# A hybrid encoder layer: the MLP's ticks taken in pairs, two strips and then four projections

## The reference, cut to what matters

```
hn = rmsnorm(x, ln1_g) * (1.0 + sc1) + sh1
z = hn @ w_in
...
o_c = stick_breaking(qc, k_all, v_all, q_pos, k_pos).reshape(b, t, GROUP_W)
...
mix = jnp.concatenate([o_a, o_b, o_c, o_d], axis=-1) @ w_out
x = x + g1 * mix
h2 = rmsnorm(x, ln2_g) * (1.0 + sc2) + sh2
x = x + g2 * (jnp.square(jax.nn.relu(h2 @ mlp_w1)) @ mlp_w2)
...
y_prompt = rmsnorm(xp, final_g)
```

## Time and profile before

| | |
|---|---|
| median of 3 runs | 3203.18 us |
| the profiled execution | 3203.64 us |
| its span, first to last instruction | 3201.8 us |
| mean granted clock of TensorE | 0.928 |
| TensorE busy | 2816.2 us (88%), 15463 matmuls |
| ScalarE, VectorE, GpSimd busy | 1556.1, 1355.5, 1718.6 us |
| last phase | from about 1100 us to the end |

### The profile page before, as it was taken

How to read it: one execution, slowest core, us unless ns; L and a number is a source line. 1 busy time by engine, 2 the same in 40 slices (tenths; PEclk the granted TensorE clock), 3 DMA queues, 4 the chain that set the end, 5 groups by cost and what they waited for, 6 DMA issues and landing times.

```text
span 3201.8 us, 41705 instructions
## 1 busy us (share of the span) xinstructions
PE 2816.2 (88%) x15463; PEld 2509.3 (78%) x15463; DVE 1355.5 (42%) x2145; ACT 1556.1 (49%) x2711; POOL 1718.6 (54%) x1063
## 2 busy tenths in 40 slices
PE   5898998998982469897899988899999989999998
PEld 1676776766461369887898988899899989999998
DVE  1262544534112426653566644566566323223222
ACT  2345454534233426653566644566567534434443
POOL 2335354443321036554665656566556666776775
PEclk8999999998975579998999999999999999999999
DMA  5236353444835234435345444545345454555542
GB/s 202 64 92 184 92 159 118 128 116 135 267 94 137 65 96 132 119 110 155 108 139 151 123 141 142 154 135 166 108 132 146 127 170 137 156 153 143 151 135 84
DMA packets 680334, 429.62 MB, mean 134 GB/s; under 512 B 38491, under 2 KB 637894, under 8 KB 680134
## 3 DMA queue, kind: packets, MB, share of 16 engines
q1 hardware_dynamic: 678054, 422.76, 45.2%
q10 hardware_dynamic: 2080, 4.19, 0.4%
HBM read 375.17 MB, written 51.59 MB: 133 GB/s over the span
## 4 chain that ended last, share of the span: by engine, by line
PE 43%; DVE 9%; ACT 5%; POOL 5%; issue 3%; DMA 2%; SPq 1%; DVEq 0%; ACTq 0%; POOLq 0%
PE t_hp L2249 7%; PE t_hp L2253 7%; PE t_hp L2250 7%; PE t_op L2280 6%; PE t_op L2282 6%; PE t_op L2281 6%; POOL t_w1l L1847 3%; DVE t_cc L2059 3%; PE t_tr L2193 1%; DVE t_lt L2058 1%; DMA t_h_lo<-o_scratch 1%; POOL t_nacc L1861 1%; DVE t_xs L2146 1%; ACT t_lt L1922 1%; DMA t_kt<-k_scratch 1%
## 5 line engine op out<-in xcount | busy, mean ns | idle before, releaser
L1847 POOL TENSOR_TENSOR t_w1l<-t_raw,t_w1h 128x1024 fp32r<-128x1024 f32 x240 | 583.6, 2432 | 644.8 <-ACT t_w1h L1942 644.5
L2249 PE MATMUL t_hp<-t_h_hi,t_w1h 128*128 128x352 f32 x1920 | 633.9, 330 | 50.4 <-DMA t_h_lo<-o_scratch 30.2
L1853 POOL TENSOR_TENSOR t_w2l<-t_raw,t_w2h 128x512 fp32r<-128x512 f32 x384 | 535.6, 1413 | 201.9 <-ACT t_w2h L1947 201.9
L2253 PE MATMUL t_hp<-t_h_lo,t_w1h 128*128 128x352 f32 x1920 | 628.3, 327 | 1.5 <-DVE t_h_lo L2111 1.5
L2250 PE MATMUL t_hp<-t_h_hi,t_w1l 128*128 128x352 f32 x1920 | 626.3, 326 | 0.0
L2280 PE MATMUL t_op<-t_g_hi,t_w2h 128*128 128x352 f32 x1536 | 508.0, 331 | 23.2 <-DVE t_xs L2146 22.9
L637 POOL TENSOR_TENSOR w_lo<-wraw,w_hi 128x1024 fp32r<-128x1024 f32 x110 | 268.0, 2437 | 480.5 <-ACT w_hi L720 480.5
L2282 PE MATMUL t_op<-t_g_hi,t_w2l 128*128 128x352 f32 x1536 | 499.4, 325 | 0.0
L2281 PE MATMUL t_op<-t_g_lo,t_w2h 128*128 128x352 f32 x1536 | 498.9, 325 | 0.0
L2249 PEld LDWEIGHTS t_hp<-t_h_hi,t_w1h 128*128 128x128 f32 x1920 | 368.9, 192 | 61.5 <-DMA t_h_lo<-o_scratch 32.3
L2250 PEld LDWEIGHTS t_hp<-t_h_hi,t_w1l 128*128 128x128 f32 x1920 | 370.2, 193 | 3.1 <-issue 0.2
(11 more groups left out here) (310 smaller groups left out, 4416.5 us busy)
## 6 DMA issues: line engine op xcount, KB each, us to landing
t_raw<-in_mlp_w_dram SPq DMA_DIRECT2D x384, 256.0 KB, 3.1
t_raw<-in_mlp_w_dram SPq DMA_DIRECT2D x192, 512.0 KB, 4.2
wraw<-in_w_in_dram SPq DMA_DIRECT2D x110, 512.0 KB, 3.9
t_raw<-in_w_out_dram SPq DMA_DIRECT2D x48, 512.0 KB, 3.8
mod_w<-in_w_ada_dram SPq DMA_DIRECT2D x8, 2048.0 KB, 9.2
t_kt<-k_scratch SPq DMA_DIRECT2D x40, 256.0 KB, 4.5
t_vt<-v_scratch SPq DMA_DIRECT2D x40, 256.0 KB, 4.6
t_xs<-x_scratch SPq DMA_DIRECT2D x6, 1408.0 KB, 8.8
```

The source lines that it names most:

```text
L1847: pool.tensor_tensor(w1l[r % W1S][:, :, :], raw1[r % RAW1][:, :, :], w1h[r % W1S][:, :, :].bitcast(F32), ALU.subtract).then_inc(w1_lo, 1)
L1853: pool.tensor_tensor(w2l[r % W2S][:, :, :], raw2[r % RAW2][:, :, :], w2h[r % W2S][:, :, :].bitcast(F32), ALU.subtract).then_inc(w2_lo, 1)
L2249: pe.matmul(bank, w1h[g % W1S][:, k, :], h_hi[:, k, :], start=(k == 0), stop=False)
L2253: ins = pe.matmul(bank, w1h[g % W1S][:, k, :], h_lo[:, k, :], start=False, stop=(k == KT - 1))
```

## The change

Only `walk` changes. In the chunks 1 to 6 of a block, projections are no longer made two at a time behind each strip, but four at a time behind each second strip, and `pace` is called with 1 after each projection instead of with 2 after each two. What the engines do in a strip, a projection, a turn or a step is unchanged, and so is the number of units in a chunk. `bank_uses` gives the same numbers as before, as projections don't use the hp banks.

```
--- before.py
+++ after.py
@@ -1534,10 +1534,10 @@
                 pace(2)
                 if m and j == 0 and 1 <= c <= len(ROWS_OF):
                     turn(m - 1, c - 1)
-                if c and not last:
-                    project(m, c - 1, 2 * j)
-                    project(m, c - 1, 2 * j + 1)
-                    pace(2)
+                if c and not last and j % 2:
+                    for d in range(4 * (j // 2), 4 * (j // 2) + 4):
+                        project(m, c - 1, d)
+                        pace(1)
             if last and m + 1 < NMB:
                 pace.finish(NEEDS[m + 1])
             for d in range(KT if last else 0):
```

## The result

The changed kernel takes 3431.34 us (median of 4 runs, 3428.32 to 3433.76) against 3203.19 us for the kernel before beside it (4 runs, 3202.19 to 3208.1): a ratio of 1.0709, 95% interval 1.069 to 1.0727, slower by 228 us. The forecast was 3457 us, the range 3335 to 3520.

The account below looks back on a forecast made before the run. TensorE's own stream was taken to set the time, every new hole adding to the end. Turns 57.9, runs of four 125.4 and clock 48.0 + 22.4 gave +253.7 on the profiled 3203.6, less 0.5: 3457 us, range 3335 to 3520.

Parts of the forecast that it names:

- turns: Strip right after a turn waits for its hp bank: 6 holes of 6.2 us behind a step, 9 of 3.2; +57.9 us.
- runs of four: Four projections on two op banks: the third waits until VectorE has added the first, late behind a step; +125.4 us.
- clock: TensorE at a lower granted clock behind holes over 2 us, 1.6 us each: 48.0 for 30 runs, 22.4 for 14 turns.
- A: Runs with a step ahead of the first projection, none ahead of second or third: 6 at 5.7, 3 at 4.2, 3 narrow at 1.5 us.
- B: Runs with a step ahead of the first and third projections: 10 at 3.8 us, 4 narrow ones at nothing.
- C: Runs with steps ahead of the first and second projections: 3 at 5.1 us, the middle between 3.8 and 2.6 more.
- D: Runs with a step ahead of the second projection alone: 8 at 2.6 us, 2 narrow ones at nothing.
- typical pair: Two projections behind a step in the earlier trace, by which a third would wait 4.2 us for the first's addition.
- Rival 4: VectorE's scan waits for whole GpSimd conversions, 0.7 us more in each of 30 runs: 3479 us; chance 0.05.
- Rival 1: Only the turns cost; additions come within one projection, so four in a run cost nothing: 3283 us; chance 0.09.
- Rival 2: TensorE's holes come as forecast but without the lower clock behind them: 3386 us; chance 0.13.
- Rivals 3 and 5: 3: steps stand more evenly, late-chain waits go, 3175 us, chance 0.03; 5: extra waits equal lost old ones, no change, 0.03.

## Why the prediction was right, and where its sizes were off

The sum against the profiled execution, 253.7 against 226.7 us:

| term | predicted | measured | from |
|---|---|---|---|
| turns | 57.9 | 57.5 | wait for t_yrow |
| runs of four | 125.4 | 110.2 | wait for the addition |
| clock | 70.4 | 72.5 | TensorE's busy time |
| other waits | 0 | -13.5 | idle time less the first two |

**Turns.** Right in mechanism and size: 6.5 behind a step in the longest case, 3.18 where no step is near, 15 in number. The earlier trace rows carried the price, because before the change the wait was there already, only covered.

**Runs of four.** Right in mechanism, the sum 14% too high; by class, added up from the timeline:

| class | runs | predicted | measured |
|---|---|---|---|
| A, step ahead of the first projection | 12 | 51.3 | 44.9 |
| B, ahead of the first and third | 14 | 38.0 | 31.7 |
| C, ahead of the first and second | 3 | 15.3 | 5.7 |
| D, ahead of the second | 10 | 20.8 | 29.3 |
| last chunks, and the rest | | 22.9 | 21.6 |

A's prices held, 5.7 behind two steps (five of six at 5.2 to 6.6) and 4.2 behind a turn (3.8 to 4.1); what it lacks is one run without a hole. The sizes that missed, in B, C and D, came from a row of the last chunk taken for a run that stands otherwise. B was priced at 3.8, the hole behind two strips with two steps; most of its runs have one step ahead, and seven lie between 2.2 and 2.8, which is the typical pair's 4.2 less the step of 1.36 that covers it. D was priced at 2.6, but it is the typical pair moved by one projection: second and third behind a step, the fourth waits; five of its eight full runs are at 3.7 to 4.4. C's bound ("at least B's") was wrong: the second step fills part of the wait and its chain comes behind the first addition, so 1.9 on average. One rule comes near most of the full runs with one step in the way: 4.2, less what TensorE does beyond one projection before it asks for the bank. It is too low behind two steps (A as above, B at 3.5 to 5.1 in three runs) and too high for C (2.8 against 1.9). One full A and one full B came out as zero: TensorE had stood 3.54 us before an attention product ahead of the A, and 5.60 us before one inside the B, and a hole that is taken once isn't taken twice.

**Clock.** 1.6 us to a hole over 2 us was right in sum, and near in its parts. With the steps off the run the waits for the addition over 2 us went from 30 to 4 and 43.9 us of busy time with them, 1.7 each (1.2 for each of all 37 holes that went). A turn came to 1.7 with the turn moved (24.8 us for 15, with new waits beside it), 1.9 in blocks 4 and 5, and 2.2 with the holes filled.

**What was put at nothing.** No wait for weights or loads came up, as said. The waits elsewhere, of which the low bound let 20 us go, did fall, by 13.5; they stand behind the same late queues as the new holes, so part of the new waiting seems only to have taken their place (the two runs without a hole above show it), and the sum should have carried it.

**Blocks 4 and 5** were to grow by 14.4 us each; they grew by 18.5 and 13.8. The 6 holes of 3.18 are there, and no wait for the addition is new; the surplus in block 4 lies in its busy time (281.2 to 289.8 us, where block 5 has 4.2 more) and in 0.5 us more of a wait for the load of t_h_lo.

**Scan and GpSimd.** Here the reading of the rows failed, without harm to the sum. The prediction took the earlier trace rows for an overlap in which both run on, each longer. The row of GpSimd merges two conversions, one of 1.3 and one of 2.2 us; taken apart, each excludes the scan, as the scan of 3.25 us in the same trace already showed. The Trainium skill (SBUF — State Buffer, section "SBUF: two separate sides") says that whichever of the two starts first holds the shared port pair for the whole instruction and blocks the other; the trace agrees (40 scans, 1.08 us behind the conversion's end), and so does the run in which the scan reads PSUM, where both fall back to 1.28 and 1.29. Rival 4 had this mechanism right and its price wrong: the 2.22 us of the row were already the wait for the rest of a conversion, so the 0.7 us a run that it added came on top of what was counted.

**The other rivals.** Rival 1 (only the turns cost) falls with the 110.2 us; VectorE has idle time, but within a step it waits for ScalarE (1.57 and 1.12 us in the hole shown above), and the addition comes behind that in its order. Rival 2 (no clock) falls with the 72.5. Rivals 3 and 5: the waits that were to pay for the change fell by 13.5, against 240.2.

## What to carry to other kernels

What two buffers between engines that work in order can bear is set by what stands ahead of the release in the releasing engine's queue, not by that engine's load: VectorE was 48% busy in blocks 1 to 3, and its late additions cost 110 us. Before regrouping work, ask of each buffer that is reused sooner what its release is queued behind, and price it by a row where that queue has the same order, not merely a similar hole. And where an operation shows two durations, take its neighbours apart one by one before calling it contention: the one operand that made the scan and the conversions take turns was worth more (26.5 us, on the unchanged order) than any reordering of steps that was tried on the kernel before.

## What the runs showed of the hardware

- A scan of 512 columns with both operands in SBUF that begins while a GpSimd conversion runs ends 1.08 us behind that conversion, whether 0.37, 1.1 or (in the kernel before) 2.17 us of it was left; with one operand in PSUM every one of the 96 takes 1.28, and the conversion beside it 1.29, so a PSUM operand costs the scan nothing (1.285 alone before). The 1024-column conversions of the first layer are freed too: their longest goes from 3.22 to 2.45 us.
- Behind a single hole of 2.48 us, ahead of which the granted clock had been 1.00 for some 7 us, it was 0.58 over the first 2.7 us, and behind the wait of 2.5 us in the kernel before 0.69; over the first 6.6 us it was 0.74 behind either. Matmuls into a free bank, read by nobody, in place of the turns' 61.2 us of waiting won 33 us in the medians.
